# A modulation table transposed in turns: identity transposes replaced by two-column matmuls, and their eviction moved from VectorE to ScalarE

## The reference, cut to what matters

```python
# first block, per layer
h = h + 0.5 * swiglu_ffn(rmsnorm(h, norm_ffn1[i]), w_ffn1_in[i], w_ffn1_out[i])
u = rmsnorm(h, norm_mix[i]) @ w_mix_in[i]
z, xbc, dt_raw, q, k, v, q_idx, k_idx, w_idx = jnp.split(u, SPLIT_POINTS, axis=-1)
y_ssd = ssd_mixer(z, xbc, dt_raw, ...)          # 16 heads of 64, decay = exp(segment sums)
y_att = dsa_mixer(q, k, v, q_idx, k_idx, w_idx, positions)   # index scores, top 64, 8 heads
h = h + jnp.concatenate([y_ssd, y_att], axis=-1) @ w_mix_out[i]
...
# second block, per layer
sh1, sc1, g1, sh2, sc2, g2 = jnp.split((silu_c @ w_mod[l] + b_mod[l])[:, None, :], 6, axis=-1)
csh1, csc1, cg1, csh2, csc2, cg2 = jnp.split(silu_cc @ w_mod[l] + b_mod[l], 6, axis=-1)
```

## Time and profile before

| | |
|---|---|
| median of 3 runs | 2906.9 us (2906.47 to 2910.42) |
| the profiled execution's own time | 2906.9 us |
| its span, first to last instruction | 2905.1 us |
| TensorE matmul busy | 2802.4 us, 96% |
| VectorE busy | 1719.8 us, 59% |
| ScalarE busy | 1158.2 us, 40% |
| mean granted TensorE clock | 0.984 |

### The profile page before, as it was taken

The page is one execution under the profiler, slowest core; times in us unless marked ns, Lnnn a source line. Parts: engine busy times, 40 slices in busy tenths (PEclk is TensorE's granted clock), DMA queues, the critical chain, the costliest instruction groups (busy, mean ns, idle before and its releaser), DMA issues.

```text
span 2905.1 us, 38014 instructions
## 1 busy us (share of the span) xinstructions
PE 2802.4 (96%) x16070; PEld 2349.9 (81%) x16070; DVE 1719.8 (59%) x2405; ACT 1158.2 (40%) x1531; POOL 387.8 (13%) x331
## 2 busy tenths in 40 slices
PE   7999999999999999999999999999999979899998
PEld 6888787888888877788879866667878869789787
DVE  7843144486784214458689753446757659655674
ACT  5431313344443121344433445524434443565442
POOL 2400010132230001013101420010000000511000
PEclk9998999999999999999999999999999989999999
DMA  7553675455555467545513222225555524343652
GB/s 229 181 190 107 191 244 189 131 189 188 174 185 178 122 202 245 167 142 192 185 56 105 84 73 73 59 83 183 188 171 176 188 72 148 103 127 117 217 181 95
DMA packets 442319, 445.09 MB, mean 153 GB/s; under 512 B 13711, under 2 KB 433672, under 8 KB 442150
## 3 DMA queue, kind: packets, MB, share of 16 engines
q1 hardware_dynamic: 438878, 436.52, 47.0%
q0 software_dynamic: 2400, 5.40, 0.9%
q10 hardware_dynamic: 872, 0.75, 0.1%
HBM read 441.46 MB, written 1.17 MB: 152 GB/s over the span
## 4 chain that ended last, share of the span: by engine, by line
PE 89%; DVE 7%; ACT 3%; DMA 1%; issue 1%; SPq 0%; ACTq 0%; DVEq 0%
PE bank L1561 29%; PE bank L1562 15%; PE bank L1660 13%; PE bank L1523 12%; PE bank L1670 8%; PE bank L1556 2%; DVE R L2571 2%; PE bank L1776 2%; PE bank L1977 1%; PE bank L1718 1%; PE bank L1968 1%; DVE lower L2121 1%; DVE lower L687 1%; ACT upper L1035 1%; PE bank L1852 1%
## 5 line engine op out<-in xcount | busy, mean ns | idle before, releaser
L1561 PE MATMUL bank<-h_pair,upper 128*128 128x512 f32 x2464 | 873.4, 399 | 31.4 <-DVE h_pair L2152 18.7
L2121 DVE TENSOR_TENSOR lower<-ring,upper 128x2048 fp32r<-128x2048 f32 (+1 forms) x238 | 567.1, 2385 | 290.7 <-ACT upper L1035 290.5
L1562 PE MATMUL bank<-h_pair,lower 128*128 128x256 f32 x2464 | 693.5, 281 | 0.0
L1035 ACT ACTIVATE upper<-ring 128x2048 fp32r<-128x2048 f32 (+1 forms) x238 | 441.4, 1863 | 473.8 <-PE bank L1562 473.7
L1561 PEld LDWEIGHTS bank<-h_pair,upper 128*128 128x128 f32 x2464 | 466.3, 189 | 144.9 <-issue 29.1
L1562 PEld LDWEIGHTS bank<-h_pair,lower 128*128 128x128 f32 x2464 | 469.4, 191 | 0.2
L1561 PE MATMUL bank<-hid_pair,upper 128*128 128x512 f32 x1232 | 431.6, 395 | 0.0
L1562 PE MATMUL bank<-hid_pair,lower 128*128 128x256 f32 x1232 | 345.1, 280 | 0.0
L1561 PEld LDWEIGHTS bank<-hid_pair,upper 128*128 128x128 f32 x1232 | 230.9, 187 | 53.8
L1660 PE MATMUL bank<-hT,ring 128*128 128x256 f32 x1152 | 256.0, 384 | 6.9 <-DVE hT L2080 6.0
L1660 PEld LDWEIGHTS bank<-hT,ring 128*128 128x128 f32 x1152 | 221.9, 193 | 39.5 <-issue 6.7
(11 more groups left out here) (311 smaller groups left out, 3674.7 us busy)
## 6 DMA issues: line engine op xcount, KB each, us to landing
ring<-in_w_ffn_in SPq DMA_DIRECT2D x154, 1024.0 KB, 5.1
ring<-in_w_ffn_out SPq DMA_DIRECT2D x56, 1024.0 KB, 4.9
ring<-in_w_mix_in SPq DMA_DIRECT2D x48, 1024.0 KB, 5.4
ring<-in_w_mod SPq DMA_DIRECT2D x48, 1024.0 KB, 5.6
ring<-in_w_in SPq DMA_DIRECT2D x42, 1024.0 KB, 5.2
ring<-in_w_ffn_out SPq DMA_DIRECT2D x28, 768.0 KB, 4.3
ring<-in_w_mix_out SPq DMA_DIRECT2D x16, 1024.0 KB, 7.0
ring<-in_w_in SPq DMA_DIRECT2D x16, 512.0 KB, 5.2
```

The source lines that it names most:

```text
L1035: act.activation(f.upper(p)[:, 0:n], slot[:, 0:n], ACT.Copy).then_inc(up_ready, 1)
L1561: pe.matmul(bank[:, 0:2 * T], up[:, cols], x_pair.rearrange("p e t -> p (e t)"), start=first, stop=False)
L1562: return pe.matmul(bank[:, 0:T], low[:, cols], x_pair[:, 0, :], start=False, stop=last)
L2121: dve.tensor_tensor(f.lower(p)[:, 0:n], slot[:, 0:n], f.upper(p)[:, 0:n].bitcast(F32), ALU.subtract)\
```

## The change

1. TensorE's eight transposes of a turn become eight matmuls: the 128 columns of `mod_rows` are the stationary operand and a new tile `mod_sum` (128 x 2) is the moving one. Column v of `mod_sum` is 1 at partitions 32j + v, so the product transposes and adds the four partial sums at once. A turn's result is 16 columns of one bank.
2. VectorE makes `mod_sum` at the start by one reduction over the identity matrix, after a wait for its load; TensorE waits for it once, after the first feed-forward stage.
3. VectorE's `turned_mod` goes with its calls. ScalarE copies the 16 columns to `modraw` in `take_fills`, in the slot's order.
4. In ScalarE's logit and head loops `take_fills(..., u - 1)` moves from ahead of the Relu or exponential of step u to behind it. In the unit loop its place is unchanged.

```diff
+        mod_sum = take(2)
...
+                        else:
+                            dst = modraw[:, (l * 96 + 16 * n):(l * 96 + 16 * n) + 16]
+                            take_item(it, [(dst, banks(it)[0][:, 0:16])])
...
                 for u in range(8):
-                    take_fills("logit", u - 1)
                     act.wait_ge(logit_filled, (l * 8 + (u + 1)))
...
                     ins.then_inc(relu_ready, 1)
+                    take_fills("logit", u - 1)
                 take_fills("logit", 7)
...
                 for h in range(SSD_H + 2):
-                    take_fills("head", h - 1)
                     if h < SSD_H:
                         act.wait_ge(seg_ready, (l * SSD_H + (h + 1)))
                         act.activation(seg[h % 2], seg[h % 2], ACT.Exp).then_inc(decay_ready, 1)
+                    take_fills("head", h - 1)
...
                 if l == 0:
                     pe.wait_ge(cc_ready, 3)
+                    pe.wait_ge(mod_sum_ready, 1)
...
                             evicted(pe, items + FILL_ITEM["mod", 4 * n + 3])
-                            bank = start_item(it)
+                            bank = start_item(it)[0]
                             for c in range(8):
-                                mm = pe.transpose(bank[c // 4][:, 128 * (c % 4):128 * (c % 4 + 1)],
-                                                  mod_rows[n % 2][:, 128 * c:128 * (c + 1)], ident[:, :])
+                                mm = pe.matmul(bank[:, 2 * c:2 * c + 2],
+                                               mod_rows[n % 2][:, 128 * c:128 * (c + 1)], mod_sum,
+                                               start=True, stop=True)
                             mm.then_inc(gemm_filled, 1)
...
             dve.memset(cc, 0.0).then_inc(cc_zeroed, 1)
+            dve.wait_ge(ident_landed, 16)
+            dve.tensor_reduce(mod_sum, ident[:, :].rearrange("p (j v) -> p v j", v=MOD_W)[:, 0:2, :], AX.X, ALU.add)\
+               .then_inc(mod_sum_ready, 1)
...
-                def turned_mod(kind, i):
...
-                        for b in range(2):
-                            at = l * 96 + 16 * n + 8 * b
-                            ins = dve.tensor_reduce(
-                                modraw[:, at:at + 8].rearrange("p (c v) -> p c v", v=2),
-                                pair[it % 2][b][:, :].rearrange("p (c j v) -> p c v j", c=4, v=MOD_W)[:, :, 0:2, :],
-                                AX.X, ALU.add)
-                        ins.then_inc(pair_free[it % 2], 1)
...
-                turned_mod("logit", 7)
...
-                    turned_mod("head", i - 1)
...
-                    turned_mod("unit", i - 1)
```

More of the change, by code:

```diff
@@ L546, in program @@
         trig_ready, angles_ready = sem("trig_ready"), sem("angles_ready")
-        cc_ready, cc_zeroed = sem("cc_ready"), sem("cc_zeroed")
+        cc_ready, cc_zeroed, mod_sum_ready = sem("cc_ready"), sem("cc_zeroed"), sem("mod_sum_ready")
         x_landed, ctx_landed = sem("x_landed"), sem("ctx_landed")
```

## The result

The changed kernel takes 3023.67 us (3018.86 to 3033.83, four runs) against 2907.44 us before, a ratio of 1.0403 (95% interval 1.0375 to 1.0431): 116 us slower. The forecast was 2980 us with a range of 2957 to 3005. The direction was right, the size was not.

What follows compares the result with a forecast made beforehand. The prediction took TensorE's own work to bound the kernel. Waits 55.0, logits 0.3, turns 8.0, ScalarE copies 0.4 and clock falls 10 made 73.7 us on 2906.9: 2980 us, range 2957 to 3005.

Steps and rivals of the forecast that it cites:

- The wait: Head loops: TensorE's fill waits for a buffer pair whose eviction now stands behind the exponential; 55.0 us for two layers.
- step 15: Last listed head step: its mod fill is free, its turn waits 0.9 us for slot 14's mod item.
- The list of steps: Head steps of a layer: ten behind a qkv item at 2.10 us, three behind a mod item at 1.87 us.
- the step without a wait (10): Head step 10 follows a slot of one item; its qkv fill needs an item evicted long before: 0.
- The turn: Eight matmuls replace eight transposes: 1.6 us a turn, +0.67 us each, 8.0 us for twelve, bounds 6.1 and 10.4.
- The row of 16 columns: Profile row used to price the turn's matmuls: two matmuls of 16 columns in 0.45 us, 0.225 us each.
- The estimate from the Trainium skill's figure for the transpose mode: Turns: transposes four times faster for FP32, so 0.47 us a matmul and +34 us for twelve turns.
- The gains: Head loop and turns: earlier exponential gives back 0; VectorE loses 24 reductions, 3.4 us busy, none awaited by TensorE: 0.
- The clock: Head loops: TensorE's clock falls around some short slots, 2.5 us a fall, 10 us in all, bounds 0 and 56.
- the eight short slots: Head slots 3, 7, 11 and 15 in two layers, where one in two was taken to bring a clock fall.
- the long steps: Head steps whose waits stand between 7 us qkv fills; most waits do, which was held against falls nearly everywhere.
- Rival 2: Head loops: the clock falls at nearly every wait, 28 in two layers, 1.6 us each: 3015 us; chance 0.12.

Runs made afterwards that it cites:

- order_filled: order_only plus four added, thrown-away matmuls of 256 columns behind each csrow but the first, filling TensorE's wait; 2965.76 us, ratio 1.0221 to the kernel before.
- order_only: The kernel before with only the new eviction order in the logit and head loops, turns still transposes; 2970.10 us, ratio 1.0232.
- turn_only: The changed kernel with the old eviction order, so only the two-column matmul turns are new; 2923.21 us, ratio 1.0069 to the kernel before.
- order_shift6: order_only with six added matmuls once a layer behind csrow 0, shifting the head loop in time; 2979.35 us in one run.
- after_shift3: The changed kernel with three added matmuls once a layer behind csrow 0, shifting the head loop in time; 3028.50 us in one run.

## Why the prediction was wrong

**The wait.** Forecast 28 waits: 2.10 us behind qkv, 1.87 behind mod, 0.9 in step 15, together 55.0 us. The trace prints 1.97 and 1.75, counted from the tail of csrow; from the moment the fill could have started it is 2.13 us (order_filled's step), so 0.16 more than printed. With 0.7 for step 15's turn that is 20 x 2.13 + 6 x 1.91 + 2 x 0.7 = 55.5 us. The list of steps, the two prices and the step without a wait (10) were right. order_only's head loops are 68.5 us longer in all, 55.5 of waits and 13 of clock.

**The turn.** Forecast +0.67 us each with bounds 0.51 and 0.87; measured 1.81 - 0.93 = 0.88, and 0.96 with the matmul behind it in the eight head turns: some 11 us for twelve, just over the upper bound of 10.4. The row of 16 columns (0.225 us a matmul) was the right one, though two columns seemed nearer to one. The estimate from the Trainium skill's figure for the transpose mode (TensorE: Matmul & The Clock Gate, Terms), 0.47 us a matmul, did not come: a matmul took 0.23 us.

**The gains.** None forecast, none came: VectorE's reductions are gone and TensorE had not waited for them, and the exponential starts no earlier than `seg` allows.

**The clock: the step that failed.** The prediction took a fall "at one in two of the eight short slots" at 2.5 us, 10 us. In place of it the head loops have 58 and 50 us at 1.2 GHz. Waits and turns explain 55.5 + 8 x 0.96 = 63.2 of the 111.5 us there; the other 48 us are the clock. (TensorE is busy for 100 us of the low stretches, and what it did there would take half of that at full clock: 50 us.) Where it went wrong is where the falls were looked for. Two passes through the first logits had one fall and a single hole of 2.5 us was read as having none, and from this the long steps, with a 7 us fill on each side, were counted as safe. In layer 0 of the changed kernel every qkv fill behind a wait of 1.97 us pays 1.76 us: the long steps, and not the short ones alone.

The reading of the earlier trace rows was itself wrong. Its window ends at 2898, 0.65 us after the hole; the clock falls at 2900.0. And the kernel before has another hole of 2.54 us, ahead of an unbroken run of matmuls, with a fall 1.1 us behind its end:

```profile
2472.19 0.39 PE L1556 MATMUL bank<-upper,h_up 128*128 128x256 f32 x1 [2.54 <-DVE lower L687]
2473.40:2476.40 3.00, 3.00 (x16) 3.00 (x15) 3.00 (x4) 2.04 (x3) 2.92 (x4) 0.50 0.24 76
2900.00:2902.00 2.00, 0.00 (x0) 0.00 (x0) 0.67 (x2) 0.69 (x1) 0.00 (x0) 0.50 0.58 217
```

(one line of TensorE's timeline, two windows). Its holes of 2.96 and 2.97 us, which end at 940.4 and 2363.4, have a fall 0.3 and 0.7 us behind them as well; one of 2.06 us, which ends at 2487.5, has none. So the trace on hand spoke against the long steps being safe. Near the end TensorE has little left to do, so what brought that fall is not shown.

Rival 2 ("the clock falls at nearly every wait", 3015 us) was the case that came, with a chance of 0.12. The Trainium skill (TensorE: Matmul & The Clock Gate, A second HAM failure mode) describes a clock that swings where TensorE idles briefly as it cycles through PSUM banks; the trace agrees, with 1.97 us of idle time and a qkv fill of 8.77 us, and low clock in all 16 head steps of layer 0 and in 14 of layer 1.

**What is shown of the cause, and what is open.** Shown: nearly all the falls need the hole (filled: 0 us of low clock with transposes, 4 and 3 us with two-column turns; half filled: 7 and 7), with transposes or 128-column turns they stay at 14 to 20 us a loop, and two-column turns raise them to 50 to 58. Shown by one run each: the length of the turn and the start of the loop do not set the amount. Open: why a two-column turn in four of sixteen steps also brings falls in steps far from it. In layer 0 of the changed kernel the falls come in series (each of steps 1, 2, 5, 6, 8, 12 and 13 pays); in layer 0 of order_only steps 2, 3, 4, 7, 14 and 15 have low clock and the others none. That a fall, by making a step longer, sets up the next hole for another is a guess that no run takes apart.

turn_only's +20 us is explained in part: some 11 us of turns and 3.4 us of clock behind the unit turns. The profiled executions differ by 13.2 us in all, the medians by 20.

## What to carry to other kernels

When two engines take turns on two buffers, an instruction moved ahead of a buffer's release costs the whole chain up to that release in every pass, however idle the engine is: look for what stands between the last reader and the next writer, not for busy time. A repeated hole of 2 us in TensorE's work can cost more than itself: price it once with the clock kept and once with a fall behind each. For evidence go through all holes of that size in the trace on hand, and read the clock for some us behind each, since the falls in the changed kernel's heads began 0.1 to 1.9 us after the hole's end. A float32 matmul with a full stationary tile took 0.23 us here for 2 moving columns and 0.24 for 128, so the wide form is nearly free, and between holes it came with a third of the low clock.

## What the runs showed of the hardware that was not expected

- 128 moving columns in place of 2 cost 0.08 us over eight matmuls (1.89 against 1.81 us) and, between holes, took 70 us of low clock off the two head loops.
- Idle holes of 1.97 us in order_only's steps brought a fall or none with the same instructions around them (fills of 7.07 and 8.76 us in steps 1 and 2), yet the low clock of a head loop repeated closely from layer to layer (order_only 14 and 14 us, order_shift6 17 and 17, after_shift3 54 and 54, the changed kernel 58 and 50).
- Outside the changed stretch the executions differ too: the first logits of layer 0 began anywhere from 310.8 to 320.6 us after the start, with 7 to 31 us of low clock before them, in kernels whose TensorE work is the same up to there. The two go together only roughly (20.5 us of low clock both with a start at 311.7 and at 320.6).
